# Head of a two-layer trunk: which queue issues the second half of the first x tile

## What is computed

```
def rms_norm(x, g):
    y = xf * lax.rsqrt(jnp.mean(xf * xf, axis=-1, keepdims=True) + EPS)
    return (y * g.astype(jnp.float32)).astype(x.dtype)

h = rms_norm(x, norm_g)
proj = h @ w_in          # D_MODEL = 1024 -> IN_COLS = 6656
```

## Time and profile before

| | us |
|---|---|
| three runs, median (lowest to highest) | 1628.51 (1628.11 to 1630.4) |
| the profiled execution, its own time | 1628.55 |
| its span in the profile | 1626.8 |
| TensorE busy | 1619.1 |
| VectorE busy | 974.7 |
| ScalarE busy | 670.9 |
| GpSimd busy | 114.7 |

### The profile page before, as it was taken

How to read it: one execution, slowest core, us unless ns; L and a number is a source line. 1 busy time by engine, 2 the same in 40 slices (tenths; PEclk the granted TensorE clock), 3 DMA queues, 4 the chain that set the end, 5 groups by cost and what they waited for, 6 DMA issues and landing times.

```text
span 1626.8 us, 19865 instructions
## 1 busy us (share of the span) xinstructions
PE 1619.1 (100%) x7516; PEld 1351.1 (83%) x7516; DVE 974.7 (60%) x1175; ACT 670.9 (41%) x805; POOL 114.7 (7%) x164
## 2 busy tenths in 40 slices
PE   9999999999999999999999999999999999999998
PEld 7888888888888888888888888888888888888887
DVE  8267876775666566534353778657766665656223
ACT  5244335532345545522233533345333555444213
POOL 4000000000310000002120000000005000000021
PEclk9999999999999999999999999999999999999999
DMA  5342222223332323233333322222233232323232
GB/s 190 103 117 78 78 78 91 78 73 96 92 102 90 103 90 103 91 99 95 98 110 105 103 78 78 79 92 76 78 93 102 92 102 90 103 90 104 91 104 78
DMA packets 44557, 154.33 MB, mean 95 GB/s; under 512 B 4944, under 2 KB 5456, under 8 KB 44496
## 3 DMA queue, kind: packets, MB, share of 16 engines
q1 hardware_dynamic: 42624, 149.12, 29.2%
q10 hardware_dynamic: 1872, 4.33, 0.9%
HBM read 149.24 MB, written 2.10 MB: 93 GB/s over the span
## 4 chain that ended last, share of the span: by engine, by line
PE 99%; DVE 0%; DMA 0%; ACT 0%; DVEq 0%; issue 0%; SPq 0%; ACTq 0%
PE ps L1009 31%; PE ps L1011 31%; PE ps L1010 31%; PE ps L1110 1%; PE ps L1099 1%; PE ps L1077 1%; PE ps L1081 1%; PE ps L1228 0%; PE ps L1121 0%; PE ps L1017 0%; PE ps L1016 0%; PE ps L1015 0%; PE ps L1064 0%; DMA xs<-xt 0%; DVE xg L686 0%; DVE xs L684 0%
## 5 line engine op out<-in xcount | busy, mean ns | idle before, releaser
L662 DVE TENSOR_TENSOR w_lo<-w_raw,w_hi 128x1024 fp32r<-128x1024 f32 x274 | 350.9, 1291 | 291.5 <-ACT w_hi L424 288.1
L1009 PE MATMUL ps<-u_hi,w_hi 128*128 128x512 f32 x1344 | 525.5, 391 | 0.0
L1011 PE MATMUL ps<-u_hi,w_lo 128*128 128x512 f32 x1344 | 523.3, 389 | 0.0
L1010 PE MATMUL ps<-u_lo,w_hi 128*128 128x512 f32 x1344 | 523.2, 389 | 0.0
L424 ACT ACTIVATE w_hi<-w_raw 128x1024 fp32r<-128x1024 f32 x274 | 286.3, 1055 | 281.7 <-DMA w_raw<-wts 275.0
L1011 PEld LDWEIGHTS ps<-u_hi,w_lo 128*128 128x128 f32 x1344 | 252.3, 188 | 53.0
L1010 PEld LDWEIGHTS ps<-u_lo,w_hi 128*128 128x128 f32 x1344 | 252.5, 188 | 50.9
L1009 PEld LDWEIGHTS ps<-u_hi,w_hi 128*128 128x128 f32 x1344 | 252.4, 188 | 50.8
L1009 PE MATMUL ps<-g_hi,w_hi 128*128 128x512 f32 x344 | 133.8, 389 | 0.0
L1010 PE MATMUL ps<-g_lo,w_hi 128*128 128x512 f32 x344 | 133.8, 389 | 0.0
L1011 PE MATMUL ps<-g_hi,w_lo 128*128 128x512 f32 x344 | 133.8, 389 | 0.0
(11 more groups left out here) (208 smaller groups left out, 2070.3 us busy)
## 6 DMA issues: line engine op xcount, KB each, us to landing
w_raw<-wts SPq DMA_DIRECT2D x274, 512.0 KB, 3.5
q<-q ACTq DMA_DIRECT2D x8, 256.0 KB, 3.5
out<-rows SPq DMA_DIRECT2D x8, 256.0 KB, 2.9
xs<-xt SPq DMA_DIRECT2D x7, 256.0 KB, 6.2
dec<-decay ACTq DMA_DIRECT2D x2, 514.0 KB, 4.7
w_raw<-wts SPq DMA_DIRECT2D x4, 256.0 KB, 5.6
cs<-rope ACTq DMA_DIRECT2D x2, 512.0 KB, 4.0
cst<-consts SPq DMA_DIRECT2D x1, 192.0 KB, 8.0
```

Source lines behind the costliest of these rows:

```text
L662: nc.vector.tensor_tensor(w_lo[:, s, :], w_raw[:, s, :], w_hi[:, s, :].bitcast(F32), ALU.subtract).then_inc(s_lo, 1)
L1009: nc.tensor.matmul(dst, a_hi, b_hi, start=start, stop=False)
L1010: nc.tensor.matmul(dst, a_hi, b_lo, start=False, stop=False)
L1011: return nc.tensor.matmul(dst, a_lo, b_hi, start=False, stop=stop)
```

## The change

The load of x0b leaves SyncE's queue and is issued by ScalarE on its own queue, directly behind x0a. SyncE goes from w0a straight to x1. The waits, the semaphores (`s_x[0]` for x0b) and all arithmetic stay as they are.

```
             def load_x(k):
-                a = KT + k * S if k else KT + S // 2
+                a = KT + k * S
                 sp.dma_start(xs[:, a:KT + (k + 1) * S], xt[:, a:KT + (k + 1) * S]).then_inc(s_x[k], 16)
 
             sp.dma_start(w_raw[:, 0, 0:HALF], wts[0, :, 0:HALF]).then_inc(s_head, 16)
-            load_x(0)
             load_x(1)
...
             act.dma_start(xs[:, 0:KT + S // 2], xt[:, 0:KT + S // 2]).then_inc(s_x0a, 16)
+            act.dma_start(xs[:, KT + S // 2:KT + S], xt[:, KT + S // 2:KT + S]).then_inc(s_x[0], 16)
             act.wait_ge(s_warm, 1)
```

## The result

| | before | changed |
|---|---|---|
| median of 19 runs, us | 1628.14 | 1631.40 |
| lowest and highest | 1627.54, 1630.40 | 1629.08, 1632.56 |
| ratio, with its 95% interval | | 1.0018 [1.0012, 1.0024] |
| the profiled execution, its own time | 1628.55 | 1630.70 |
| its span | 1626.8 | 1628.9 |

The change makes the kernel slower by about 3 us, 2.0 to 3.9 by the interval, which is 0.2% of the time. I had forecast 0.3 us faster, in a range up to 1629.5; the result is above the range and of the other sign.

A forecast was written before the change was run, and what follows sets the result against it. TensorE's dense stretch, started by x0b's landing, bounds the kernel; 0.4 us gained there and 0.3 at VectorE put slab 3 at 22.07, 0.3 us earlier: 1628.55 to 1628.25, median forecast 1628.2 us, range 1627.5 to 1629.5.

The forecast's parts named there:

- What bounds the kernel: Head: TensorE, dense from 6.80 to 1617 us, bounds the kernel; its start there is set by x0b landing at 5.59.
- The issue: Head: x0b still goes out at about 1.2, no gain; x1, w0b and the rest are issued 0.45 us earlier.
- the cover of 1.11 us: ScalarE: w_hi of w0a waited 1.11 us for data, so the second issue's 0.42 us delay costs nothing.
- The landing of x0b: Head, ScalarE's queue: x0b lands at 5.2 us, between 4.9 and 5.45, so TensorE starts 0.4 us earlier.
- the hole: Loads, 3.8 to 4.5 us: the core moves only 94 GB/s, 58 packets; the missing 0.17 MB are 0.5 us.
- The slow end: Head: taking turns one to one, x0b and x1 end together at 6.85, 1.26 us later than x0b before.
- With x1 on another queue this hole can be filled: Loads, 3.8 to 4.5 us: x1 no longer waits behind x0b's slow packets, which helps x1 more than x0b.
- The slower rival: Head: x0b shares with x1 and lands at 6.3 to 6.85, giving 1629.1 to 1629.6 us; chance 0.20.
- Each 0.1 us on it is 0.1 us on TensorE's start: Head: x0b's landing moves TensorE's start into its dense stretch one for one; 1.21 us lie between landing and 6.80.
- What is late next: Slab 3: VectorE's low part ends at 22.33, TensorE's weight load starts at 22.37, so TensorE's gain needs VectorE to move too.
- The term d: VectorE before slab 3: its shift from earlier loads, taken as 0.3 us earlier, between 0 and 0.5.
- A measurement of this kernel tells 0.2%, 3.3 us: Whole kernel: only changes of 0.2%, 3.3 us, can be told from none; same got 0.95, slower 0.03, faster 0.02.

## Why the prediction was wrong

- **What bounds the kernel**: right. TensorE is dense from the u_lo matmuls on, and what came late there came late at the end (2.8 of 3.1 us).
- **The issue**: right. x0b goes out at 1.21, the table load moves by 0.48 us, and the cover of 1.11 us still has 0.90 left. But w0a itself came 0.26 us later, which I had not foreseen; it stays hidden behind x0b.
- **The landing of x0b**: this step failed. I said "I take 5.2 us, the middle of 4.9 and 5.45", from rates of 237 and 347 GB/s. It landed at 7.07, even beyond the end of 6.85 that I had from turns with x1. Both rates came from other stretches, before and after the hole; from 4 to 5.6 us, with x0b in flight on ScalarE's queue, the core moved 132 GB/s. The slow end was too low as it took x1's old landing for fixed; u_hi of x1 itself came 0.18 us later.
- **"With x1 on another queue this hole can be filled"**: wrong. The hole is some 80 packets a us before (58 in 0.7 us) and 100 after, and it lasts longer; on two queues the packets are divided one to one from 4 to 5.6 us, and x0b gets half of them. The slower rival had the lateness from sharing, with rows 6 for it. The run in which TensorE keeps its pace, 1629.15 with 13 warm-ups, falls in its price of 1629.1 to 1629.6, but that is in part luck: for a landing at 7.17 its own sum gives 1.58 - 0.14 = 1.44 us, which is 1629.95. I gave it 0.20, weighing a hole that seemed to leave room above the row on turns.
- **"Each 0.1 us on it is 0.1 us on TensorE's start"**: true of the start, not of the end. I wrote that the largest loss that rows bound is 1.3 us. The term left out, put at nothing without a reason, is TensorE's pace: the matmuls that took 4.67 us took 6.29, at half the clock, behind 1.73 us of idle time in place of 0.50. The working had the idle time (0.50 us in rows 3) and never asked what else it might cost. With this term the slower rival would have read 1630.7 to 1631.2, and a range that takes it in would have come near 1631.4.
- **What is late next**: slab 3 was named rightly as the place that takes a gain back, but there was no gain. Here it gave 0.3 us back, of which I had named 0.14. The term d, 0.3 us that VectorE was to gain from earlier loads, had the wrong sign: VectorE starts on slab 3 0.50 us later.
- **"A measurement of this kernel tells 0.2%, 3.3 us"**: too coarse. The interval here, 2.0 to 3.9 us, tells the change from none, though the median moved by less than 3.3.

## What to carry to other kernels

Moving an urgent load to a second queue did not put it ahead of the first queue's loads here; it made it share with them, and with 2 KB rows beside its 1 KB rows it landed 1.5 us later. If the first queue has the load in front, leave it there; short rows beside it took half of the lateness away, and holding the others back took all of it, yet left the time 1.8 to 2.7 us over the kernel before. In a head that is padded with warm-up work, look at TensorE's pace behind the wait and not at the wait alone: a load late by 1.5 us cost 3 us here, and five more warm-up matmuls gave more than half of it back without touching a load.

## What the runs showed of the hardware

- A load of 128 rows of 1 KB landed at 4.77 with nothing behind w0a on the queue beside it, at 5.59 ahead of x1 on the same queue, at 6.13 behind x1 on the same queue (issued 0.5 us later there), at 6.33 and 6.31 beside 1 KB rows on the other queue, and at 7.07, 7.17 and 7.16 beside 2 KB rows there.
- TensorE lost 1.6 us to its clock after 1.73 us without work, about as much (1.6 us in the medians) after 0.96 us without work behind a shorter warm-up, and 1.16 us of pace after no more than 0.34 us without work in the kernel with x1 ahead of x0b. In the first the granted clock showed it, 0.50 from 9 to 12 us; in the other two the matmuls ran at half pace with 1.00 in that column.
- With a shorter lateness than the changed kernel's, executions of one kernel fall in two groups some 2 us apart (x1 in halves: 1628.0 to 1629.0 and 1630.2 to 1630.4; x0 in one load likewise), so a median hides a mixture. A longer warm-up left one main group both times (1627.41 to 1628.48; 1627.92 to 1628.69 and one run at 1629.47).
- In four of these kernels the traffic sank some 3 us after a stream of issues began, to 83, 98, 85 and 151 packets a us, where the kernel before has 190 from 5.6 us on. Pausing the issues moved this. Its cause was not found.
